# Moving the eight complex tables of an S5 mixer from GpSimd to VectorE, and the copy of u from VectorE to ScalarE

## What is computed

```
hn = rms_norm(h, norm_mix[l])
proj = hn @ w_in[l]
u_ssm = proj[..., :D_SSM]
q = proj[..., D_SSM:D_SSM + D_ATTN]          # then k, then v
# s5_mixer, for each of 32 groups of 16 channels with 64 complex states:
bu_re = jnp.einsum('btgc,gnc->btgn', ug, bb_re.astype(dt_))
bu_im = jnp.einsum('btgc,gnc->btgn', ug, bb_im.astype(dt_))
_, _, s_re, s_im = lax.associative_scan(combine, (a_re_t, a_im_t, bu_re, bu_im), axis=1)
y = (jnp.einsum('gcn,btgn->btgc', c_re.astype(dt_), s_re)
     - jnp.einsum('gcn,btgn->btgc', c_im.astype(dt_), s_im))
```

## Time and profile before

| | us |
|---|---|
| median of three runs | 671.12 (670.17 to 671.66) |
| the profiled execution | 670.81 |
| its span | 668.8 |
| PE busy | 656.2 (98%) |
| DVE busy | 487.2 (73%) |
| ACT busy | 340.6 (51%) |
| POOL busy | 172.5 (26%) |

### The profile page before, as it was taken

The page is one execution under the profiler, slowest core; times in us unless marked ns, Lnnn a source line. Parts: engine busy times, 40 slices in busy tenths (PEclk is TensorE's granted clock), DMA queues, the critical chain, the costliest instruction groups (busy, mean ns, idle before and its releaser), DMA issues.

```text
span 668.8 us, 10548 instructions
## 1 busy us (share of the span) xinstructions
PE 656.2 (98%) x3914; PEld 542.1 (81%) x3914; DVE 487.2 (73%) x801; ACT 340.6 (51%) x587; POOL 172.5 (26%) x177
## 2 busy tenths in 40 slices
PE   8899999999999999999999999999999999999997
PEld 7688778877888788887998888888888888888886
DVE  5998998578766665557697666666656687868967
ACT  6538564766745464764354333334334345554662
POOL 4998992223220102330000111011110121100000
PEclk9999999999999999999999999999999999999999
DMA  8868515666120404030357555564566446655663
GB/s 296 309 206 130 167 44 145 177 185 221 64 66 1 158 2 188 4 124 0 127 189 249 199 182 188 192 225 151 186 222 218 151 170 223 211 189 140 182 196 125
DMA packets 67737, 106.99 MB, mean 160 GB/s; under 512 B 15792, under 2 KB 40496, under 8 KB 66288
## 3 DMA queue, kind: packets, MB, share of 16 engines
q1 hardware_dynamic: 64528, 100.17, 45.9%
q10 hardware_dynamic: 3168, 6.29, 2.9%
HBM read 89.54 MB, written 15.73 MB: 157 GB/s over the span
## 4 chain that ended last, share of the span: by engine, by line
PE 80%; DVE 11%; ACT 3%; SPq 2%; DMA 2%; issue 1%; POOL 1%; ACTq 0%; DVEq 0%
PE pb L510 23%; PE pb L512 23%; PE pb L511 23%; PE pb L1962 6%; PE pb L1965 4%; DVE F L1384 3%; DVE wring L500 2%; ACT F L993 1%; DMA raw<-in_w_in 1%; SPq L664 1%; DMA F<-scr_y 1%; DVE F L1390 1%; DVE pb L1384 1%; DVE sq L1432 1%; DVE wring L1384 1%
## 5 line engine op out<-in xcount | busy, mean ns | idle before, releaser
L510 PE MATMUL pb<-xs,wring 128*128 128x512 f32 (+1 forms) x400 | 149.6, 374 | 0.7 <-POOL xs L911 0.7
L512 PE MATMUL pb<-xs,wring 128*128 128x512 f32 (+1 forms) x400 | 148.9, 372 | 0.0
L511 PE MATMUL pb<-xs,wring 128*128 128x512 f32 (+1 forms) x400 | 148.9, 372 | 0.0
L1390 DVE SCALAR_TENSOR_TENSOR F<-pb,cols,F 128x511 f32<-128x511 f32 x88 | 65.9, 748 | 71.6 <-ACT F L993 69.7
L500 DVE TENSOR_TENSOR wring<-raw,wring 128x1024 fp32r<-128x1024 f32 x70 | 93.4, 1336 | 8.0 <-ACT wring L489 7.9
L510 PE MATMUL pb<-wring,xs 128*128 128x512 f32 x240 | 98.5, 411 | 0.3 <-DVE wring L503 0.3
L993 ACT ACTIVATE F<-pb,cols 128x512 f32<-128x512 f32 x50 | 38.2, 767 | 115.3 <-PE pb L512 115.2
L512 PE MATMUL pb<-wring,xs 128*128 128x512 f32 x240 | 93.9, 391 | 0.0
L511 PE MATMUL pb<-wring,xs 128*128 128x512 f32 x240 | 93.7, 390 | 0.0
L510 PEld LDWEIGHTS pb<-xs,wring 128*128 128x128 f32 x400 | 75.3, 188 | 14.1 <-issue 1.3
L512 PEld LDWEIGHTS pb<-xs,wring 128*128 128x128 f32 x400 | 75.3, 188 | 13.2
(11 more groups left out here) (152 smaller groups left out, 1011.1 us busy)
## 6 DMA issues: line engine op xcount, KB each, us to landing
raw<-in_ffn_w_up SPq DMA_DIRECT2D x22, 1024.0 KB, 5.3
F<-in_ffn_w_down SPq DMA_DIRECT2D x11, 1024.0 KB, 4.9
scr_w<-F SPq DMA_DIRECT2D x11, 1024.0 KB, 3.9
F<-in_x SPq DMA_DIRECT2D x8, 512.0 KB, 8.6
raw<-in_w_in ACTq DMA_DIRECT2D x4, 1024.0 KB, 6.3
raw<-in_w_out SPq DMA_DIRECT2D x4, 1024.0 KB, 4.9
raw<-scr_w SPq DMA_DIRECT2D x8, 512.0 KB, 3.8
raw<-scr_w SPq DMA_DIRECT2D x15, 256.0 KB, 4.7
```

The lines of the kernel that those rows point to most:

```text
L510: nc.tensor.matmul(ps, lh, rh, start=first, stop=False)
L511: nc.tensor.matmul(ps, lh, rl_, start=False, stop=False)
L512: return nc.tensor.matmul(ps, ll, rh, start=False, stop=last)
L1390: return V.scalar_tensor_tensor(out=o, in0=a, scalar=s1, in1=b, op0=o1, op1=o2)
```

## The change

- POOL no longer makes any table. It still makes the powers' sums (`ps`), the sums of B and C, and the inverse roots.
- DVE makes all eight, in its own order: w1p_table(0) ahead of the low part of unit 5, ca_table(0) ahead of unit 7's, w1p_table(1) ahead of scan(0), ca_table(1) behind it, the tables of quarter 2 behind the low part of unit 12, those of quarter 3 behind scan(2).
- u is copied out of PSUM by ACT, four copies right behind the high part of unit 5; DVE multiplies it by `xbc` in SBUF afterwards (`u_scale`), tile 0 ahead of turns(1) and tiles 1 to 3 behind it. A new semaphore `u_ready` counts the multiplied tiles; the transfers of u to HBM and ACT's reading of q wait for it.
- On PE the factor transposes move from between u's tiles 1 and 2 to behind the first tile of unit 4.
- scan(1) stands ahead of the low part of unit 11.

```diff
@@ sync
-                after_drain(sync, f"u{q}")
+                sync.wait_ge(u_ready, q + 1)
@@ gpsimd: table, w1p_table and ca_table leave, and with them
-            w1p_table(0)
...
-            ca_table(3)
@@ scalar
             split_hi(act, U_Q + 1)
+            for m in range(4):
+                drained(A_(steps_first(uT[:, m, :]), by_step(read(act, f"u{m}")[:, :]), ACT.Copy), f"u{m}")
             drained(A_(steps_first(xbc), by_step(read(act, "xb")[:, :]), ACT.Copy), "xb")
...
-            after_drain(act, "u3")
+            act.wait_ge(u_ready, 4)
             rows("q", qk)
@@ vector
             root("x", xr_ready)
             split_lo(dve, U_Q)
+            def table(q, n, v, v_sum, v_dif, o, sign):
...
+                tt(t1, by_power[0], re, ALU.mult)
+                tt(o[1], by_power[1], dif, ALU.mult)
+                link(tt(t2, by_power[2], both, ALU.mult))
+                tt(o[0], t1, t2, ALU.subtract)
+                return tt(o[1], o[1], t1, sign)
+            def u_scale(m):
+                after_drain(dve, f"u{m}")
                 if m == 0:
                     after_drain(dve, "xb")
-                drained(tt(steps_first(uT[:, m, :]), by_step(p[:, :]), steps_first(xbc), ALU.mult), f"u{m}")
-            for m in range(4):
-                u_evac(m)
+                tt(uT[:, m, :], uT[:, m, :], xbc, ALU.mult).then_inc(u_ready, 1)
+            u_scale(0)
             turns(1)
+            for m in range(1, 4):
+                u_scale(m)
+            w1p_table(0)
             split_lo(dve, U_Q + 1)
             split_lo(dve, U_Q + 2)
             turns(2)
+            ca_table(0)
             split_lo(dve, U_Q + 3)
             turns(3)
...
+            w1p_table(1)
             scan(0)
+            ca_table(1)
             split_lo(dve, 9)
             head_event("q", qk, range(TT), H, "q")
             split_lo(dve, 10)
             head_rows("q", qk, range(TT), H, HD)
+            scan(1)
             split_lo(dve, 11)
-            scan(1)
             split_lo(dve, 12)
+            w1p_table(2)
+            ca_table(2)
...
             scan(2)
+            w1p_table(3)
+            ca_table(3)
@@ tensor
-                            if m == 1:
-                                pe.wait_ge(xr_ready, 1)
-                                token_factors("xb", "x")
-            proj(4, U_Q, "q")
+            for t in range(TT):
+                proj_tile(4, U_Q, "q", t)
+                if t == 0:
+                    pe.wait_ge(xr_ready, 1)
+                    token_factors("xb", "x")
```

More of the change, by code:

```diff
@@ L213, in layer @@
         piece_in = [sem(f"piece_in{i}") for i in range(len(PIECES))]
+        u_ready = sem("u_ready")
         k_hi, u_hi, u_lo, x0_in = sem("k_hi"), sem("u_hi"), sem("u_lo"), sem("x0_in")
@@ L858, in _ @@
             pool.wait_ge(pw_ready, 1)
[L860 to L883, removed]
             nc.gpsimd.tensor_tensor(ps[:, :, :], pw[:, 0], pw[:, 1], ALU.add).then_inc(sums_ok, 1)
-            pool.wait_ge(sums_ok, 3)
-            w1p_table(0)
             pool.wait_ge(c_in, 16)
@@ L890, in _ @@
             sub(cmat[:, 2], cmat[:, 0], cmat[:, 1]).then_inc(sums_ok, 1)
-            pool.wait_ge(sums_ok, 4)
-            ca_table(0)
             pow_event(EVN["mem"])
[L894 to L902, removed]
-            ca_table(3)
             pow_event(EVN["k"])
@@ L1538, in _ @@
             split_lo(dve, U_Q)
[L1540 to L1544, removed]
+            def table(q, n, v, v_sum, v_dif, o, sign):
+                g0 = q * QP
+                shape = [128, QP, n, CG]
+                t1, t2 = (ptmp[:, i, 0:QP * n * CG].rearrange("p (a b c) -> p a b c", a=QP, b=n) for i in range(2))
+                o = [a.rearrange("p (a b c) -> p a b c", a=QP, b=n) for a in o]
+                by_power = [a[:, g0:g0 + QP, 0:n].unsqueeze(3).to_broadcast(shape) for a in (ps, pw[:, 0], pw[:, 1])]
+                re, dif, both = (a[:, g0:g0 + QP, :].unsqueeze(2).to_broadcast(shape) for a in (v, v_dif, v_sum))
+                tt(t1, by_power[0], re, ALU.mult)
[3 more added lines that the diff above has]
+                return tt(o[1], o[1], t1, sign)
@@ new lines, in w1p_table, with ca_table @@
+            def w1p_table(q):
+                if q == 0:
+                    dve.wait_ge(sums_ok, 3)
+                if q == 3:
+                    read(dve, "w1r0")
+                    read(dve, "w1i0")
+                table(q, L, bb[:, 0], bc[:, 0], bc[:, 1], [w1p[q][:, i, :] for i in range(2)], ALU.add).then_inc(w1p_ready, 1)
+                dve.wait_ge(w1p_ready, q + 1)
+            def ca_table(q):
+                if q == 0:
+                    dve.wait_ge(sums_ok, 4)
+                if q >= 2:
+                    after_drain(dve, f"yo{q - 2}")
+                table(q, L + 1, cmat[:, 0], bc[:, 2], cmat[:, 2], [ca[:, q % 2, i, :] for i in range(2)], ALU.subtract)\
+                    .then_inc(ca_ready, 1)
+                dve.wait_ge(ca_ready, q + 1)
```

## The result

The change makes the kernel slower: 681.21 us (median of four runs, 678.67 to 684.09) against 670.88 for the kernel before (four runs, 670.17 to 671.66), a ratio of 1.0155 with the 95% interval 1.0112 to 1.0198. The forecast was 677.7 with a range of 674.0 to 680.8: the direction was right, the size 3.5 us short, and the time lies 0.4 us outside the range.

A forecast was written before the change was run, and what follows sets the result against it. TensorE binds (98% busy), with VectorE level as second bound from 33.3 us on. +7.5 us at kernels_in(1) less 0.9 for the scan wait gives +6.6 on 670.8, 677.4; median 0.3 above, 677.7, range 674.0 to 680.8.

The forecast's parts named there:

- The wait for the factors: Before unit 4: TensorE still waits from 30.25, unit 4 starts at 32.6 instead of 34.65, 2.05 us won.
- VectorE up to unit 5: VectorE from 35.3: 9.1 us of work, so TensorE waits 6 us and unit 5 starts 4.3 us later.
- The price of the tables: From 44.4 us: mean squares of q's heads at about 73.0, kernels_in(1) at 76.2, TensorE 7.5 us late.
- The relief of 6 us: VectorE up to q's mean squares: its other operations get shorter without GpSimd beside them, counted in full.
- full lock: Port pair shared by VectorE and GpSimd, locked for all operations: relief some 3 us more, time 674.7.
- What comes back: At outputs(1): scan(1) is sooner relative to TensorE, its wait of 0.92 is gone, TensorE 6.6 us late.
- The other four tables: 13.5 us more on VectorE between 87 and 117 us; costs nothing, 1.5 us at most.
- The clock: Step from profiled execution to the runs' median: 0.3 us added.
- Rival 3: Clock falls more often, at the first wait (before unit 4) or at kernels_in(1): 679.1 to 681.0; chance 0.21.
- Rivals 1, 2 and 4: VectorE keeps ahead at unit 5, 668.1, chance 0.07; only the first wait, 674.1, 0.17; no difference, 671, 0.05.

The follow-up runs named there:

- low15_first: Changed kernel with m_lo and the low part of unit 15 ahead of quarter 3's tables on VectorE: 680.71 us.
- late_half: Kernel before with only the tables of quarters 2 and 3 on VectorE, behind the low parts of units 12 and 15: 671.98 us.
- loads_later: Changed kernel with ScalarE's loads of chunks 7 and 9 issued behind the work that stood behind them: 682.15 us.
- low5_first: Changed kernel with the low part of unit 5 ahead of u_scale(0) on VectorE: 681.45 us.
- root_later: Changed kernel with ScalarE's y_out(0) ahead of q's inverse root: 682.15 us.
- tables_only: Kernel before with the eight tables on VectorE at the changed kernel's places; u, transposes and second scan as before: 678.81 us.
- repaired: Changed kernel; low part of unit 5 before u, y_out(0) before q's root, unit 11's before scan(1), m_lo and unit 15's before quarter 3's tables: 678.66 us.
- root_behind_repaired: repaired with q's inverse root behind kernels_in(1) on ScalarE instead of only behind y_out(0): 674.88 us.

## Why the prediction was wrong in size

Two terms of its sum failed, both put at next to nothing: what the tables of quarters 2 and 3 cost behind 90 us, and what a falling clock adds to the median. The rest held within 0.8 us.

- **The wait for the factors**: right. Unit 4 at 32.36 (forecast 32.6). That the clock would stay up in this wait holds for the trace of the changed kernel, not for all: of the four experiments that equal it up to 60 us, the clock fell there in three (waits of 2.21, 2.46 and 2.74 us; unit 5 at 44.72, 45.10, 45.41) and not in one (1.91 us; 43.83).
- **VectorE up to unit 5**: right. u starts at 35.19 (35.3), unit 5 at 44.12 (44.4), the wait 5.54 (6). The tensor_scalar of 1024 columns was 0.69 us, not 0.9.
- **The price of the tables**: right. q's mean squares end at 73.08 (73.0), kernels_in(1) at 76.52 (76.2 to 76.4). The relief of 6 us, taken from the pairs of the earlier trace rows, came in full; the 3 us more that a full lock would have given back did not show.
- **What comes back**: right in kind. outputs(1) is 7.4 us late (forecast 6.6), because of a new wait of 0.73 for chunk 7's load, behind the low part of unit 11, which the change moved behind scan(1). The wait for the scan is gone as forecast.
- **"The other four tables... Nothing at these places, 1.5 us at most"**: wrong, and the first of two steps that failed. The low part of unit 15 was reckoned against its reader on PE, with 0.5 us to spare, and PE indeed never waits for it. It has a second reader: the load of chunk 9 on ScalarE's queue waits for the buffer, and ScalarE's copies stand behind the load. At its place this costs 3.0 us by low15_first (38.0 against 35.0 us between the same two pieces, waits of 0.59 and 2.20 among them). In the kernel's time it is less, as 2.3 us of PE's lateness came back by the end, 0.7 net in this trace. The same four tables have a third way to PE that the prediction did not list, over SyncE's issues of y behind the low part of unit 17 and scan(3): late_half, which moves only these tables, loses 2.2 us by it, and low15_first loses as much once chunk 9 is in time. So the mechanism was wrong, and the term was not nothing: 0.7 us by the end of the changed kernel's trace, which is inside the 1.5 allowed, and 2.2 where it was measured by itself, which isn't.
- **The clock**: the second step that failed, and the larger one. The sum added 0.3 us from the profiled execution to the median, and it was 2.5. Of the 3.5 us by which the forecast was short, 2.2 are this, and 1.3 lie in the profiled execution (678.67 against 677.4). By these numbers either miss alone would have left the time inside the range. Rival 3 named the mechanism and carried 0.21, at the first wait and at kernels_in(1); the forecast should have had a part of it in its own sum, as a wait of over 2 us was forecast twice. Its first place fits the experiments, as said above. Its second does not: loads_later and low15_first waited 1.94 and 2.38 us there and kept the clock. It fell instead at k's first transposes in four traces, behind waits of 1.97, 1.99, 2.12 and 3.24 us (low5_first, root_later, tables_only, loads_later).
- **The sum as measured**: 6.6 + 0.8 (outputs(1)) + 3.0 (chunk 9) - 2.3 (back) = 8.1 of span, and 2.5 of clock on the runs. That the clock accounts for the 2.5 is worked out from the runs' spans: 679.8 us at 0.990 against 676.9 at 0.994 is 0.004 of 677 us, 5.4 us more at half speed, thus 2.7 us, for 2.9 measured; the other two runs come out at 4.7 for 5.4 (0.987) and 2.7 for 1.8 (0.990). At which place it fell in those runs no trace shows.
- Rivals 1, 2 and 4 fell with unit 5 at 44.12 and the wait at kernels_in(1).

## What to carry to other kernels

Work moved to an engine whose results gate others costs more by its place in the queue than by its amount: eight tables, 27 us of VectorE, stood in one order at +10 us and in another at +5 (+3 with u left as it was). None of the orders reached zero. For every low part, buffer or result that is delayed, list all its readers, the DMA issues on other engines' queues too, and what stands behind those issues. When one such wait is mended, look for the chain that ended just behind it, for it takes the place. And where a forecast puts a wait of about two microseconds or more on TensorE, put the half clock behind it into the sum with its chance.

## What the runs showed of the hardware

- A VectorE product of 128x512 takes 0.62 us with one input in PSUM, whether GpSimd works (before) or not (tables_only; four in 2.48 in both), and 1.63 us with both inputs in SBUF while GpSimd makes products (three in 4.90), against 0.63 with GpSimd idle (three in 1.90).
- A tensor_scalar of 1024 columns in SBUF took 0.69 us alone, 1.12 and 1.55 beside GpSimd; a product of the same width 1.22. The Trainium skill, in "VectorE: DVE Perf Modes", section "Mode 2×_2P — use both read ports for one tensor", has single-source operations fetch two elements of a tensor at once; the ratio of 0.69 to 1.22 agrees.
- Waits of PE of much the same length did and didn't bring the granted clock down: 1.91, 1.94, 2.10, 2.20, 2.38, 2.39 and 2.40 us did not, 1.97, 1.99, 2.12, 2.21, 2.46, 2.58, 2.59, 2.74 and 2.76 did. A wait of 1.89 us at unit 7 stands in three traces; the clock fell in one (low5_first) and not in the other two (repaired, root_behind_repaired). The lengths overlap, so the length of a wait alone doesn't tell.
- A load issued by ScalarE holds up ScalarE's own copies while it waits for its buffer: 7.13 and 7.24 us of standing still in the changed kernel ahead of two issues of 0.37 us. Standing still is not yet a cost: the kernel before has 6.58 us of it ahead of chunk 7's load too, and there PE does not wait.
- SyncE's queue does the same to its own issues: in late_half y's write at 121.85 stands right behind a load at 121.41 that waited for a low part, where the kernel before has the two at 115.72 and 115.28.
